# Seven products of halves for two channel tiles in the input projection of a long-convolution block

## What is computed

```python
def _hyena(h, w_in, b_in, conv_w, conv_b, ...):
    u = _centred_conv3(h @ w_in + b_in, conv_w, conv_b)   # h: 1024 x 1024, w_in: 1024 x 3072
    v, x1, x2 = jnp.split(u, 3, -1)
    kf = _hyena_filters(L, ...)                           # filters of the two long convolutions
    z = x1 * long_conv(v, 0)
    z = x2 * long_conv(z, 1)
    return z @ w_out + b_out
```

## Time and profile before

| | before |
|---|---|
| median of 3 runs | 3907.69 us (3905.93 to 3911.46) |
| profiled execution, its own time | 3907.51 us |
| its span | 3905.7 us |
| TensorE matmuls busy | 3610.5 us (92%) |
| TensorE weight loads busy | 2233.3 us (57%) |
| VectorE busy | 2554.0 us (65%) |
| ScalarE busy | 884.7 us (23%) |
| GpSimd busy | 461.4 us (12%) |
| granted TensorE clock, mean | 0.967 of full speed |

### The profile page before, as it was taken

One profiled execution on the slowest core, in us unless ns is written; L12 is line 12 of the kernel. 1 busy time (PEld: TensorE's weight loads), 2 busy tenths in 40 slices (PEclk: granted clock), 3 DMA queues, 4 the chain that ended last, 5 costly groups with the idle time before them and its releaser, 6 DMA issues. The chain is left out here.

```text
span 3905.7 us, 63530 instructions
## 1 busy us (share of the span) xinstructions
PE 3610.5 (92%) x26142; PEld 2233.3 (57%) x26142; DVE 2554.0 (65%) x3451; ACT 884.7 (23%) x1758; POOL 461.4 (12%) x499
## 2 busy tenths in 40 slices
PE   6999989998879999999999998999976998868996
PEld 3444478884455555555555555544455898435563
DVE  5656379995876666767666674454076778557773
ACT  2000022221122221222212112322135443113232
POOL 0000000003100000000000001000031876001110
PEclk9999999998989999999999999999987999989998
DMA  7573322216589999999999995211002100228996
GB/s 278 218 261 138 143 76 109 117 76 239 219 285 361 335 328 327 326 335 329 328 328 333 332 325 205 89 56 70 33 1 90 37 4 4 100 92 315 357 357 226
DMA packets 289975, 798.58 MB, mean 204 GB/s; under 512 B 18728, under 2 KB 25904, under 8 KB 275120
## 3 DMA queue, kind: packets, MB, share of 16 engines
q1 hardware_dynamic: 271856, 719.02, 50.5%
q0 software_dynamic: 17136, 73.54, 5.9%
q10 hardware_dynamic: 720, 2.17, 0.2%
HBM read 708.56 MB, written 86.11 MB: 203 GB/s over the span
## 5 line engine op out<-in xcount | busy, mean ns | idle before, releaser
L1550 PE MATMUL banks<-moe_down,moe_hidT 128*128 128x512 f32 x1280 | 565.7, 595 | 9.4 <-DMA moe_down<-d_wd 9.3
L1550 PEld LDWEIGHTS banks<-moe_down,moe_hidT 128*128 128x128 f32 x1280 | 237.6, 191 | 281.5 <-issue 276.1
L1920 PE MATMUL banks<-hT,w_in_ring 128*128 128x512 f32 (+3 forms) x976 | 363.9, 535 | 1.9 <-ACT hT L1981 1.0
L518 PE MATMUL banks<-hT,w_in_ring 128*128 128x512 f32 x768 | 339.3, 596 | 1.4 <-PEq L212 1.4
L1623 ACT COPY moe_parts<-banks 128x512 f32<-128x512 f32 (+1 forms) x240 | 123.4, 514 | 840.7 <-PE banks L1529 837.7
L1529 PE MATMUL banks<-moe_wsums,moe_xsums 128*64 128x256 f32 x2560 | 301.3, 389 | 8.1 <-DVE moe_xsums L1667 4.0
L1920 PEld LDWEIGHTS banks<-hT,w_in_ring 128*128 128x128 f32 (+1 forms) x976 | 183.2, 188 | 180.7 <-issue 170.2
L1529 PEld LDWEIGHTS banks<-moe_wsums,moe_xsums 128*64 128x64 f32 x2560 | 181.1, 139 | 134.5 <-issue 49.1
L518 PEld LDWEIGHTS banks<-hT,w_in_ring 128*128 128x128 f32 x768 | 142.8, 190 | 185.2 <-issue 175.7
L757 PE MATMUL banks<-x_block,dft 128*128 128x256 f32 x896 | 196.5, 382 | 6.3 <-PEq L392 6.3
L757 PEld LDWEIGHTS banks<-x_block,dft 128*128 128x128 f32 x896 | 171.6, 192 | 30.3 <-issue 6.7
(11 more groups left out here) (479 smaller groups left out, 6015.8 us busy)
## 6 DMA issues: line engine op xcount, KB each, us to landing
moe_down<-d_wd SPq DMA_DIRECT2D x160, 1024.0 KB, 11.1
x_block<-d_wg SPq DMA_DIRECT2D x96, 1024.0 KB, 7.9
x_block<-d_wu SPq DMA_DIRECT2D x96, 1024.0 KB, 10.9
mix<-d_wg SPq DMA_DIRECT2D x64, 1024.0 KB, 8.8
mix<-d_wu SPq DMA_DIRECT2D x64, 1024.0 KB, 11.3
x_block<-d_seq SPq DMA_DIRECT2D x19, 1024.0 KB, 4.8
w_in_ring<-d_w_in SPq DMA_DIRECT2D x9, 2048.0 KB, 10.1
x_block<-d_mod_w SPq DMA_DIRECT2D x8, 2048.0 KB, 11.9
```

The lines of the kernel that those rows point to most:

```text
L518: last = nc.tensor.matmul(m.ps[:, g % 2, :], ring[:, c, k, (mt % 4) * P:(mt % 4 + 1) * P], hT[:, k, h * BANK:(h + 1) * BANK], start=(k == ...
L1550: last = nc.tensor.matmul(m.ps[:, Y_BANK + h, :], hidT[:, j % 2, i * P:(i + 1) * P], wd[:, i, h * BANK:(h + 1) * BANK], start=(fc == 0 and ...
L1920: last = nc.tensor.matmul(m.ps[0:width, g % 6, 0:n], ring[:, q % 2, k, at:at + width], hT[:, k, first:first + n], start=(k == 0), stop=(k ...
```

## The change

Two channel tiles and two halves of the tokens make a product of 2 x 2 blocks, where the input channels are cut in two halves as well. Before, it takes eight products of halves (4 matmuls each). The change makes it with seven products and sums of blocks, a form of Strassen's method. `P1` and `P2` give the first block as before. The others use sums of the token blocks (`t1` to `t4`, made once on VectorE, in the place of `hT`'s second quarter, in `x_block` and in a new buffer) and sums of the weight blocks (four for each pair, made on GpSimd inside `w_in_ring` and in `w_diff`). The products go to three banks in turn: 0, 1 and 5; bank 5 was one of the two for transposes, which now have bank 4 alone. ScalarE evacuates `P1` and `P7` of a pair; VectorE adds the other five to blocks of `u_padded` with six adds, and GpSimd adds one block of `u_padded` to another. The loop runs over 12 pairs in place of 24 units. The modulation weights come in 24 slots of 1 MB, four to a pair in pairs 0 to 5, since their ring shrinks from four to two tiles of `x_block`. The window has one buffer in place of two and is loaded behind the last windowed product of an iteration. `magnitudes` is cut in two (`larger` and the sum). The early load of the taps waits for the last product, since the sums of tokens lie in its place.

The diff, cut to its core:

```diff
--- before.py
+++ after.py
@@ -180,8 +180,12 @@
     b, w3 = j % 2, filter_weights(m)
     for a in range(2):
         sp.dma_start(w3[a * FW:(a + 1) * FW, b], m.dram["f_w3"][:, :, j * Q:(j + 1) * Q]).then_inc((m.ahead.w3_0, m.ahead.w3_1)[b], 16)
-    sp.dma_start(m.window[:, b], m.dram["window"][j % NQ]).then_inc((m.ahead.win0, m.ahead.win1)[b], 16)
     sp.dma_start(m.f_bias[:, b, :], m.dram["f_bias"][:, j * Q:(j + 1) * Q]).then_inc((m.ahead.direct0, m.ahead.direct1)[b], 16)
+def load_window(sp, m, j):
+
+    sp.dma_start(m.window[:], m.dram["window"][j % NQ]).then_inc(m.ahead.win, 16)
...
+        b11, b12, b21, b22 = (hT[:, a * KH:(a + 1) * KH, h * BANK:(h + 1) * BANK] for a in range(2) for h in range(2))
+        t2 = in_x(4, 2).rearrange("p (k n) -> p k n", n=BANK)
+        t4 = in_x(6, 2).rearrange("p (k n) -> p k n", n=BANK)
+        t1 = b12
+
+        def a_part(n, i, a):
+            c, at = n // 2 % 2, (2 * (n % 2) + i) * P
+            return ring[:, c, a * KH:(a + 1) * KH, at:at + P]
+
+        P1, P2, P6, P7, P5, P3, P4 = range(7)
+        done = lambda n, product: 7 * n + product + 1
+        SUM_BANKS, TURN_BANK = (0, 1, 5), 4
+        bank_of = lambda n, product: SUM_BANKS[(7 * n + product) % 3]
+        u_part = lambda i, h: ub[:, i, 1 + h * BANK:1 + (h + 1) * BANK]
...
+            def next_mv(n, part):
+                for x in slots_of(n, part):
+                    if x + 2 < N_SLOTS:
+                        sp.wait_ge(s.mv_mm, x + 1)
+                        load_mv(x + 2)

             load_mv(0)
             load_mv(1)
-            for unit in range(UNITS):
-                kind, mt = unit // MT, unit % MT
-                if 2 <= unit <= 2 * N_IT and unit % 2 == 0:
-                    j = unit // 2 - 1
+            for n in range(PAIRS_IN):
+                next_mv(n, 0)
+                next_mv(n, 1)
+                if 1 <= n <= N_IT:
+                    j = n - 1
                     sp.wait_ge(s.taps, j + 1)
                     sp.dma_start(m.dram["taps"][j], taps[:, j % 2]).then_inc(kept[j % 2], 16)
                     if j + 2 < N_IT:
                         load_filter(sp, m, j + 2)
-                if unit == 2 * N_IT + 1:
+                if n + 1 < N_IT:
+                    sp.wait_ge(s.gen_read, 8 * (n + 1))
+                    load_window(sp, m, n + 1)
+                if n == N_IT:
                     for b in range(2):
                         sp.wait_ge(kept[b], NQ * 16)
                     sp.dma_start(m.dft[:], m.dram["dft"]).then_inc(s.tables, 16)
-                if mt % 4 == 3 and kind + 1 < KINDS:
-                    sp.wait_ge(s.u_mm, 2 * unit + 2)
-                    load_input_chunk(sp, m, kind + 1, mt // 4)
-                n = slot_of(unit)
-                if n is not None and n + 2 < N_SLOTS:
-                    sp.wait_ge(s.mv_mm, n + 1)
-                    load_mv(n + 2)
+                kind, c = n // 4, n // 2 % 2
+                if n % 2 == 1 and kind + 1 < KINDS:
...
+            def weight_sums(n):
+                kind, c = n // 4, n // 2 % 2
+                a11, a12, a21, a22 = (a_part(n, i, a) for i in range(2) for a in range(2))
+                if n % 2 == 0:
+                    pool.wait_ge(ready[c], (kind + 1) * 16)
+                if n:
+                    pool.wait_ge(s.u_mm, done(n - 1, P7))
+                nc.gpsimd.tensor_tensor(s3[:], a11, a21, ALU.subtract).then_inc(s.w_sums, 1)
+                pool.wait_ge(s.w_sums, 4 * n + 1)
+                nc.gpsimd.tensor_tensor(a21, a21, a22, ALU.add).then_inc(s.w_sums, 1)
+                pool.wait_ge(s.w_sums, 4 * n + 2)
+                pool.wait_ge(s.u_mm, done(n, P1))
+                nc.gpsimd.tensor_tensor(a11, a21, a11, ALU.subtract).then_inc(s.w_sums, 1)
+                pool.wait_ge(s.w_sums, 4 * n + 3)
+                pool.wait_ge(s.u_mm, done(n, P2))
+                nc.gpsimd.tensor_tensor(a12, a12, a11, ALU.subtract).then_inc(s.w_sums, 1)
+
+            def store(n):
+                pool.wait_ge(s.staged, 4 * (n + 1))
+                pool.dma_start(m.dram["seq"][n], stage[:, n % 2]).then_inc(stored[n % 2], 16)
+
+            for n in range(PAIRS_IN):
+                weight_sums(n)
+                pool.wait_ge(s.third_kept, n + 1)
+                pool.wait_ge(s.q, n + 1)
+                nc.gpsimd.tensor_tensor(u_part(1, 0), u_part(1, 0), u_part(0, 1), ALU.add).then_inc(s.z_sum, 1)
+                if n:
+                    store(n - 1)
+            store(PAIRS_IN - 1)
...
+            def product(n, which, w, x):
+                for k in range(KH):
+                    last = nc.tensor.matmul(m.ps[:, bank_of(n, which), :], w[:, k, :], x[:, k, :], start=(k == 0), stop=(k == KH - 1))
+                last.then_inc(s.u_mm, 1)
+
+            for n in range(PAIRS_IN):
+                a11, a12, a21, a22 = (a_part(n, i, a) for i in range(2) for a in range(2))
+                if n % 2 == 0:
+                    pe.wait_ge(ready[n // 2 % 2], (n // 4 + 1) * 16)
+                if n:
+                    pe.wait_ge(s.w, n)
+                    pe.wait_ge(s.c22, n)
+                product(n, P1, a11, b11)
+                if n:
+                    pe.wait_ge(s.u_ready0, n)
+                product(n, P2, a12, b21)
+                if n < N_IT:
+                    filter_pair(4 * n)
+                for x in slots_of(n, 0):
+                    matvec_slot(x)
+                if n == 0:
+                    pe.wait_ge(s.token_sums, 2)
+                pe.wait_ge(s.w_sums, 4 * n + 3)
+                if n:
+                    pe.wait_ge(s.u_ready1, n)
+                product(n, P6, a11, t2)
+                if n < N_IT:
+                    filter_pair(4 * n + 1)
+                if n:
+                    turn(n - 1, 0, 0)
+                pe.wait_ge(s.first_kept, n + 1)
+                product(n, P7, s3, t3)
+                if n:
+                    turn(n - 1, 0, 1)
+                if n == 0:
+                    pe.wait_ge(s.token_sums, 4)
+                pe.wait_ge(s.c11, n + 1)
+                product(n, P5, a21, t1)
+                if n:
+                    turn(n - 1, 1, 0)
+                before = 4 * n - 1
+                if 0 <= before < N_SLOTS and before % KT == KT - 1:
+                    pe.wait_ge(s.taps, n - 1)
+                    matvec_columns(before // KT)
+                if 1 <= n <= N_IT:
+                    norms(n - 1)
+                if n < N_IT:
+                    filter_pair(4 * n + 2)
+                for x in slots_of(n, 1):
+                    matvec_slot(x)
+                pe.wait_ge(s.w_sums, 4 * n + 4)
+                pe.wait_ge(s.q, n + 1)
+                product(n, P3, a12, b22)
+                if n:
+                    turn(n - 1, 1, 1)
+                if n < N_IT:
+                    filter_pair(4 * n + 3)
+                pe.wait_ge(s.third_kept, n + 1)
+                product(n, P4, a22, t4)
+            for i in range(2):
+                for par in range(2):
+                    turn(PAIRS_IN - 1, i, par)

...
+            b_at = COLS["b_in"][0]
+            act.wait_ge(s.bias_diff, 1)
+            for n in range(PAIRS_IN):
+                act.wait_ge(s.u_mm, done(n, P1))
+                if n:
+                    act.wait_ge(s.conv, 2 * n - 1)
+                nc.scalar.activation(u_part(0, 1), m.ps[:, bank_of(n, P1), :], ACT.Identity,
+                                     bias=m.cols[:, b_at + 2 * n:b_at + 2 * n + 1]).then_inc(s.first_kept, 1)
+                act.wait_ge(s.u_mm, done(n, P7))
+                if n:
+                    act.wait_ge(s.conv, 2 * n)
+                nc.scalar.activation(u_part(1, 0), m.ps[:, bank_of(n, P7), :], ACT.Identity,
+                                     bias=bias_diff[:, n:n + 1]).then_inc(s.third_kept, 1)
+                if slots_of(n, 1) and slots_of(n, 1)[-1] % KT == KT - 1:
...
+            nc.vector.tensor_tensor(t3[:], b22, b12, ALU.subtract).then_inc(s.token_sums, 1)
+            v.wait_ge(s.token_sums, 1)
+            nc.vector.tensor_tensor(t2, t3[:], b11, ALU.add).then_inc(s.token_sums, 1)
+            v.wait_ge(s.token_sums, 2)
+            nc.vector.tensor_tensor(t1, b12, b11, ALU.subtract).then_inc(s.token_sums, 1)
+            nc.vector.tensor_tensor(t4, b21, t2, ALU.subtract).then_inc(s.token_sums, 1)
+            in_at = COLS["b_in"][0]
+            nc.vector.tensor_tensor(bias_diff[:], m.cols[:, in_at + 1:in_at + KINDS * KT:2], m.cols[:, in_at:in_at + KINDS * KT:2],
...
+            def added(n, product, out, kept):
+                v.wait_ge(s.u_mm, done(n, product))
+                return nc.vector.tensor_tensor(out, m.ps[:, bank_of(n, product), :], kept, ALU.add)
...
+            gen = Steps(v, s.pair)
+            sum_diff(0)
+            v.wait_ge(s.pads, 2)
+            for n in range(PAIRS_IN):
+                v.wait_ge(s.first_kept, n + 1)
+                if n:
+                    v.wait_ge(s.conv, 2 * n - 1)
```

(43 more changed lines are left out.)

199 lines of the change are left out of this document (75 added, 124 removed).

## The result

The changed kernel takes **3921.88 us** (median of 9 runs, 3916.03 to 3932.27), the kernel before 3908.82 in the same series: a ratio of 1.0033 with a 95% interval of 1.0023 to 1.0043, so 13.1 us slower. The forecast was 3921, with a chance of 0.55 for slower. The profiled execution took 3923.0 us, with a span of 3921.2 and a mean granted clock of 0.964; TensorE's matmuls are busy 3580.9 us, 29.6 less than before, and VectorE 2628.7, 74.7 more.

The account below looks back on a forecast made before the run. TensorE alone was taken to pace the stage before the change. Terms -41.2 + 30 + 10.8 + 6.4 + 2 + 3 + 2.5 = +13.5 on 3907.7 gave 3921 us; 8-in-10 range 3885 to 3938.

Parts of the forecast that it names:

- pairs 2 to 5, the loop: Taps store, filter weights, weight sums, convolutions up to next direct: 44.5 us against TensorE's 37.0, four times, 30 us lost.
- pairs 6 and 7, the loop: Same loop for loads issued in pairs 5 and 6, no mod loads ahead: 39.3 us twice, 10.8 us lost.
- start, idle: Stage start: TensorE waits for filter weights behind VectorE's token sums and GpSimd's weight sums, 6.4 us idle.
- start, lower clock: After the idle stretch at the start TensorE runs four us at half speed, losing 2 us.
- lock in pairs 6 to 8: VectorE and GpSimd exclude each other on their SBUF interface, about 1.2 us a pair, 3 us in all.
- end: Stage end: one transpose bank, so an add, a convolution and three transpose-and-copy rounds follow in series: 2.5 us more.
- VectorE's leg: Loop part from the filter-weight sums through VectorE's work up to the next direct: 28.5 us.
- The transfer's leg: Loop part from the taps' store until filter weights land, behind mod loads and taps, beside GpSimd's store: 16.0 us.
- the mod loads cost nothing: Rival: transfer leg only 11 to 12 us, so the loop's 30 becomes 11, 3902 us; chance 0.2.
- The queues: Packet-by-packet turns would give GpSimd's store half the rate: loops with mod loads some 2 us longer, 3929 in all.
- GpSimd holds VectorE in every pair: Rival: GpSimd's five operations each block VectorE's leg, 2 us more in each of six loops, 3933 us; chance 0.12.
- The weights in time: Rival: small filter-weight loads pass the large ones, the loop is gone, 21.8 us saved, 3886 us; chance 0.15.

Follow-up runs that it names:

- e1: Changed kernel with the filter weights of iteration n+2 issued at the top of pair n, no longer behind the taps' store: 3882.83 us.
- e3: Changed kernel with the filter weights issued just before the taps' store instead of just behind it, mod loads still ahead of both: 3881.71 us.
- e9: Changed kernel with the next pair's filter-weight sums on VectorE behind both convolutions instead of ahead of them: 3901.68 us.
- e2: Changed kernel with the mod loads of the pair's second half issued behind the taps' store and filter weights: 3902.12 us.
- e7: Changed kernel with GpSimd's weight sums cut to 128 of 512 columns from pair 1 on, so results differ from the reference: 3921.04 us.
- e8: Changed kernel with early filter weights, first filter-weight sums before token sums, four banks for last transposes, plus window loaded in halves: 3869.07 us.

## Why the prediction was right

The sum was +13.5 and the medians say +13.1. The mechanism is the forecast's; that the number agrees to 0.4 us is partly luck, since several terms were off by more and made up for each other. By the prediction's own terms, forecast and measured in the trace of the change, with TensorE's own pace taken from e1, where the loop is open:

| term | forecast | measured | from |
|---|---|---|---|
| 48 matmuls of 512 columns | -41.2 | -41.2 | pairs 9 and 10 take 25.9 each, as worked out |
| pairs 2 to 5, the loop | +30 | +33.4 | 180.5 less e1's 147.1 |
| pairs 6 and 7, the loop | +10.8 | +6.6, lock included | 76.8 less e1's 70.2 |
| start, idle | +6.4 | +6.9 | 6.88 |
| start, lower clock | +2 | +1.3 | 2.10 and 2.41 for 1.25 and 1.92 |
| lock in pairs 6 to 8 | +3 | in the 6.6 | steps of VectorE 1.2 us longer in pair 6, 1.1 in pair 7 |
| end | +2.5 | +3.3 | 16.7 against 13.4 |

The measured terms make 10.3 of the stage's 13.1; the 2.8 left were not taken apart. The lock shows in pair 8 as well, in two steps of 2.17 us at 390.13 and 395.17.

- **The loop** is the mechanism, shown by three kernels that open it in three ways (e1, e3, e9), and by e2, which only shortens it. VectorE's leg came as worked out in the mean, 28.4, 28.7, 29.9 and 27.3 for 28.5. The second and the third hold 1.4 and 1.8 us of the lower clock (last section), measured against the same legs in e7, 27.3 and 28.1; that was no part of the working.
- **The transfer's leg** came to 16.4, 17.3, 16.1 and 16.5 us for 16.0, but the parts were mis-sized and made up for each other. I took 10.6 for the leg without mod loads and 1.4 more for GpSimd's store, 12.0 in all, and 4 for the mod loads. The runs say 9.7 with the store in it (168.99 to 178.65 in e2) and 6.3 to 7.6 for the mod loads: the 1.5 us by which they are issued earlier let little of them through. The store was 1.8 to 2.6. On the rival that the mod loads cost nothing, 3902, e2 gives the answer: it is the time the kernel has when they stand behind, 3902.12. That the numbers agree is luck too: the leg was 9.7 where the rival had 11 to 12, and a lock took 1.8 us a pair back.
- **Pairs 6 and 7.** The prediction took a transfer leg of 10.8 us there, though its own terms, 10.6 and 1.4 for the store, make 12.0. It was 8.6 and 9.4. VectorE's legs were 29.1 and 29.6, the lock in them. And TensorE's pace was put at 35.1 and 32.7, 67.8 together; e1 takes 70.2, with two waits of 0.7 in them. So 10.8 became 6.6.
- **The queues.** By the Trainium skill (DMA: Bandwidth & Descriptors, Queues, rings and completion order) each DMA engine takes turns between the rows that have work, a packet at a time. I set 2 us a loop, and 3929, against that. The store's price of 1.8 to 2.6 us for 1 MB is about what this megabyte takes at the rate of the queues in this leg, 2.4 to 2.8: six of the seven stretches of 2 us from 174 to 188 show 372 to 438 GB/s. That fits such turns, and the loop has 45.1 us, not the 46.5 behind 3929: the store costs its own bytes, not half the queue's rate for the whole leg. No run here tells turns from another way of sharing.
- **GpSimd holds VectorE in every pair**, 3933: refuted by e7. The six adds were as exempt as the Trainium skill (SBUF — State Buffer, Who interferes with whom) would have it; all 72 of them took 676 to 694 ns, as the row of the line shows (min, median and max); the one at 398.57, for instance, lies inside a GpSimd sum that runs from 398.26 to 399.78:

```profile
L726 DVE TENSOR_TENSOR u_padded<-banks,u_padded x72: 676/685/694, 71.8 to 498.3; 128x512 f32<-128x512 f32 x72
```

- **The weights in time**, 3886: this was e1's arrangement, and it measured 3882.83, so the price of the other terms was some 3 us too high; the 5.5 us for the windows are the one that e8 found to be nothing.
- **The start.** I had two of GpSimd's sums in the way and an end at 13.3 us after the stage's start; it was 13.9, and by another road. All four sums ran there, in turn with VectorE's. Timeline of GpSimd, then of VectorE, in the change:

```profile
57.78 3.34 POOL L492 TENSOR_TENSOR w_diff<-w_in_ring 128x512 f32<-128x512 f32 x1 [57.32 <-POOLq L216]
61.21 3.19 POOL L494 TENSOR_TENSOR w_in_ring<-w_in_ring 128x512 f32<-128x512 f32 x1
```

```profile
57.71 2.29 DVE L651 TENSOR_TENSOR token_diff<-hT 128x2048 f32<-128x2048 f32 x1 [0.76 <-PEq L216]
...
60.03 3.24 DVE L655 TENSOR_TENSOR x_block<-token_diff,hT 128x2048 f32<-128x2048 f32 x1
63.31 3.24 DVE L657 TENSOR_TENSOR hT<-hT 128x2048 f32<-128x2048 f32 x1
```

The last three token sums take 3.24 to 3.35 us where the first takes 2.29, and GpSimd's sums 3.2 where they take 1.26 to 1.29 alone: each operation's time holds the wait for the other's.
